# Expert gates applied to rows as they leave PSUM, and expert outputs added into x by accumulating DMAs

## The reference

```
def hier_moe(h, w_rg, w_re, w_gate, w_up, w_down):
    ...
    top_v, top_j = lax.top_k(le_g, TOPK_IN_GROUP)
    gates = p_grp[:, None] * jax.nn.softmax(top_v, axis=-1)
    expert_id = g_sel[:, None].astype(jnp.int32) * EXPERTS_PER_GROUP + top_j.astype(jnp.int32)
    return routed_experts(xt, expert_id, gates, w_gate, w_up, w_down).reshape(B, T, D)

def routed_experts(xt, expert_id, gates, w_gate, w_up, w_down):
    ...
        return (jax.nn.silu(xb @ w_gate[e]) * (xb @ w_up[e])) @ w_down[e]
    ...
    y_assign = y_rows[dest] * gate_sorted[:, None].astype(y_rows.dtype)
    return jnp.zeros_like(xt).at[tok_sorted].add(y_assign)

# per layer:  x = x + hier_moe(rmsnorm(x, norm_ffn[layer]), ...)      at the end:  y = rmsnorm(x, norm_final)
```

## Time and profile before

| | us |
|---|---|
| median of three timed runs (1150.72 to 1150.90) | 1150.72 |
| the profiled execution | 1152.18 |
| its span, first to last instruction | 1150.3 |
| PE busy (4396 matmuls) | 926.5 |
| DVE busy | 358.8 |
| ACT busy | 279.5 |
| POOL busy (266 instructions) | 203.9 |

### The profile page before, as it was taken

The page is one execution under the profiler, slowest core; times in us unless marked ns, Lnnn a source line. Parts: engine busy times, 40 slices in busy tenths (PEclk is TensorE's granted clock), DMA queues, the critical chain, the costliest instruction groups (busy, mean ns, idle before and its releaser), DMA issues.

```text
span 1150.3 us, 12314 instructions
## 1 busy us (share of the span) xinstructions
PE 926.5 (81%) x4396; PEld 510.1 (44%) x4396; DVE 358.8 (31%) x903; ACT 279.5 (24%) x590; POOL 203.9 (18%) x266
## 2 busy tenths in 40 slices
PE   6999979999829987887837998999749978778750
PEld 4566545455514432332315776877524433233220
DVE  3048994443351111000129139202431110010017
ACT  4132234455311111111125322332201111011012
POOL 0000810000011211111133433550011221111110
PEclk9999999999959999988977999999859998998995
DMA  8210143300469999999973420242569999999936
GB/s 274 74 58 1 58 147 128 141 19 20 189 254 367 362 420 422 420 422 420 413 267 99 151 80 9 74 146 111 225 269 412 379 418 421 421 421 419 386 132 238
DMA packets 66679, 278.65 MB, mean 242 GB/s; under 512 B 15837, under 2 KB 22877, under 8 KB 40138
## 3 DMA queue, kind: packets, MB, share of 16 engines
q1 hardware_dynamic: 56842, 259.16, 57.1%
q0 software_dynamic: 9792, 18.90, 4.4%
HBM read 268.76 MB, written 26.03 MB: 256 GB/s over the span
## 4 chain that ended last, share of the span: by engine, by line
PE 56%; DMA 23%; DVE 9%; ACT 4%; POOL 4%; issue 3%; SPq 1%; POOLq 0%; ACTq 0%; DVEq 0%
DMA ring<-in_moe_w_up 20%; PE bank L1599 15%; PE bank L1323 12%; PE bank L1334 11%; PE bank L1300 5%; PE bank L1612 4%; PE bank L1382 3%; PE bank L1446 1%; PE bank L1494 1%; POOL mid L545 1%; DVE x L1237 1%; DVE mid L954 1%; SPq L361 1%; PE bank L1461 1%; ACT mid L652 1%
## 5 line engine op out<-in xcount | busy, mean ns | idle before, releaser
L1599 PE MATMUL bank<-ring,mid 128*64 128x512 f32 x992 | 242.9, 646 | 61.5 <-DMA ring<-in_moe_w_up 57.6
L1599 PEld LDWEIGHTS bank<-ring,mid 128*64 128x64 f32 x992 | 81.9, 149 | 219.3 <-issue 205.7
L652 ACT ACTIVATE mid<-bank 128x512 f32<-128x512 f32 (+6 forms) x182 | 84.7, 508 | 265.1 <-PE bank L1612 124.1
L1300 PE MATMUL bank<-con,mid 128*128 128x128 f32 (+3 forms) x654 | 102.4, 297 | 53.9 <-DVE mid L954 37.7
L1300 PEld LDWEIGHTS bank<-con,mid 128*128 128x128 f32 (+3 forms) x654 | 85.2, 186 | 101.0 <-issue 50.3
L1612 PE MATMUL bank<-ring,mid 128*64 128x512 f32 x496 | 113.3, 597 | 18.6 <-issue 12.9
L1206 DVE TENSOR_TENSOR mid<-mid,bank 128x256 f32<-128x256 f32 x32 | 13.5, 421 | 310.0 <-ACT mid L849 310.0
L1334 PE MATMUL bank<-dw,hT 128*128 128x402 f32 (+1 forms) x384 | 106.3, 461 | 0.6 <-PE bank L1334 0.6
L1323 PE MATMUL bank<-dw_high,hT_high 128*128 128x512 f32 (+1 forms) x240 | 95.9, 399 | 2.6 <-POOL dw_low L582 1.7
L1323 PE MATMUL bank<-dw_low,hT_high 128*128 128x512 f32 (+1 forms) x240 | 94.1, 392 | 0.0
L1323 PE MATMUL bank<-dw_high,hT_low 128*128 128x512 f32 (+1 forms) x240 | 93.9, 391 | 0.0
(11 more groups left out here) (181 smaller groups left out, 951.7 us busy)
## 6 DMA issues: line engine op xcount, KB each, us to landing
ring<-in_moe_w_gate SPq DMA_DIRECT2D x62, 1024.0 KB, 13.1
ring<-in_moe_w_up SPq DMA_DIRECT2D x62, 1024.0 KB, 16.5
ring<-in_moe_w_down SPq DMA_DIRECT2D x62, 1024.0 KB, 18.4
dw<-in_gm_w_in SPq DMA_DIRECT2D x4, 2048.0 KB, 20.0
ring<-y_rows SPq DMA_DIRECT2D x8, 1024.0 KB, 8.0
dw<-in_par_w_in SPq DMA_DIRECT2D x4, 1608.0 KB, 9.1
dw<-in_par_w_out SPq DMA_DIRECT2D x2, 2048.0 KB, 8.4
hT<-in_moe_w_down SPq DMA_DIRECT2D x4, 1024.0 KB, 11.2
```

The costliest lines, as they stand in the source:

```text
L652: return act.activation(dst, src, ACT.Copy, scale=scale)
L1300: return pe.transpose(dst, src, ident[0:k, 0:k])
L1599: ins = pe.matmul(ps[2 + b][64 * k:64 * k + 64, :].rearrange("p (w n) -> p w n", w=2), xT[:, b, c, 64 * k:64 * k + 64], w[:, k, :, c, :], ...
```

## The change

Gates now go in where a pair leaves PSUM, and the combine is left to DMAs:

- SP's `store_gates(l)` writes `gates` to HBM (`gate_rows`, two floats a row, the order of `y_rows`), from SBUF in runs of 8 bytes. It stands between `third_pair`'s two halves in layer 0 and behind them in layer 1.
- POOL gathers for each pair the 128 gates of its slots (4 bytes each) into `gp[:, b]`, with the same index as the scatter's (`gate_index`, `gather_gates`). For the first two pairs it waits for the store; in the loop these stand behind the scatter.
- DVE's copy of `yb` becomes a multiplication by `gp[:, b]`, ACT's copy takes it as its scale; both wait for that gather (`s_gp`).
- SP's loads of `y_rows` go. POOL issues two accumulating DMAs for each tile of x, which add the rows of `y_rows` for choice 0 and for choice 1 into x in SBUF; the second of a tile waits for the first. DVE's `combine` only waits for both and counts `s_res`.
- In an overflow pair POOL gathers the next one's gates after its scatter has landed, and waits for them.

The diff, without declarations:

```diff
@@ -416,11 +423,12 @@
                 sp.wait_ge(s_dwf, 6 * (l + 1) + 1 - k)
                 gate_ups(l, 4, wgu[2], s_wgu[l][2], (k,))
 
-            def combine(l):
-                sp.wait_ge(s_moe[l], 1)
-                for j in range(NT):
-                    sp.dma_start(cb[0:ROWS[j], j], y_rows[l][2 * T0[j]:2 * (T0[j] + ROWS[j]), :]
-                                 .rearrange("(p k) n -> p k n", k=2)).then_inc(s_cl[j], 16)
+            def store_gates(l):
+                sp.wait_ge(s_gat, l + 1)
+                sp.dma_start(gate_rows[l][0:2 * TP, :].rearrange("(j p k) o -> p j (k o)", p=P, k=2), gates[:, 0:4, :],
+                             allow_slow_non_contiguous=True).then_inc(s_gst, 16)
+                sp.dma_start(gate_rows[l][2 * TP:2 * T, :].rearrange("(p k) o -> p (k o)", k=2), gates[0:TS, 4, :],
+                             allow_slow_non_contiguous=True).then_inc(s_gst, 16)
 
             sp.dma_start(x[:, 0, :], a["x_prompt"][0, 0:P, :]).then_inc(s_xl[0], 16)
             load_gain(0)
@@ -469,12 +477,13 @@
             store_rows(1, 0, range(4, NT))
             gate_ups(0, 2, wgu[1], s_wgu[0][1], (1,))
             third_pair(0, 1)
+            store_gates(0)
             for b in range(2):
                 sp.wait_ge(s_xg[0][b], 16)
             third_pair(0, 0)
             load_gain(2)
             experts(0)
-            combine(0)
+            sp.wait_ge(s_moe[0], 1)
 
             for b in range(2):
                 sp.dma_start(*((lng, a["gm_ln_g"][0].partition_broadcast(P)) if b else
@@ -500,13 +509,13 @@
             store_rows(3, 1, range(3, NT))
             gate_ups(1, 2, wgu[1], s_wgu[1][1], (0,))
             third_pair(1, 0)
+            store_gates(1)
             for b in range(2):
                 sp.wait_ge(s_xg[1][b], 16)
             gate_ups(1, 2, wgu[1], s_wgu[1][1], (1,))
             downs(1, 4, wdn[2], s_wd[1][2])
             load_gain(4)
             experts(1)
-            combine(1)
             for j in range(NT):
                 sp.wait_ge(s_h, 4 * NT + j + 1)
                 dst = out[0][0, T0[j]:T0[j] + P, :] if j < 4 else out[1][0]
@@ -530,6 +539,7 @@
             pool.memset(eps[:, 1:2], 1e-5).then_inc(s_eps, 1)
             link(pool.memset(cell[:, :], 0.0))
             pool.memset(line[:, :, 0:HIST], 0.0).then_inc(s_pz, 1)
+            link(pool.memset(gp[:, :, :], 0.0))
 
             link(pool.memset(index[:, 0, 0:P], 0.0))
             pool.memset(index[0:64, 0, 64:P], FAR).then_inc(s_m0, 1)
@@ -568,6 +578,14 @@
                 pool.indirect_dma_start(xg[:, b, :], None, h_rows[l], bass.IndirectOffsetOnAxis(ap=gix[:, b, 0:1], axis=0),
                                         bounds_check=T - 1, oob_is_err=False).then_inc(signal or s_xg[l][b], 16)
 
+            def gate_index(l, i, b):
+                pool.tensor_copy(pix[:, b, :], tab[:, bass.ds(i, 1), :].rearrange("p a v -> p (a v)")).then_inc(s_gcr[l], 1)
+                carry(s_gcr[l], 2 * l, 2 * i + 1)
+
+            def gather_gates(l, b, signal, at):
+                pool.indirect_dma_start(gp[:, b, :], None, gate_rows[l], bass.IndirectOffsetOnAxis(ap=at[:, b, 1:2], axis=0),
+                                        bounds_check=2 * T - 1, oob_is_err=False).then_inc(signal, 16)
+
             def scatter(l, i, b, n):
                 pool.wait_ge(s_yea, i + 1 + PAIRS * l)
                 pool.wait_ge(s_yed, i + 1 + PAIRS * l)
@@ -594,16 +612,24 @@
                 pool.wait_ge(s_tp, NT * (2 * l + 2))
                 gather(l, 0, 0, 0)
                 gather(l, 1, 1, 1)
+                pool.wait_ge(s_gst, 32 * (l + 1))
+                for b in range(2):
+                    gate_index(l, b, b)
+                    gather_gates(l, b, s_gp[b], pix)
 
                 def step(i, b):
                     gather(l, i + 2, b, 2 * i + 2, i + 1)
                     scatter(l, i, b, 2 * i + 3)
+                    gate_index(l, i + 2, b)
+                    gather_gates(l, b, s_gp[b], pix)
 
                 with pool.Fori(0, PAIRS // 2 - 1) as r:
                     step(2 * r, 0)
                     step(2 * r + 1, 1)
                 gather(l, PAIRS, 0, 2 * PAIRS - 2, PAIRS - 1, o_xg[l])
                 scatter(l, PAIRS - 2, 0, 2 * PAIRS - 1)
+                gate_index(l, PAIRS, 0)
+                gather_gates(l, 0, o_gp[l], pix)
                 scatter(l, PAIRS - 1, 1, 2 * PAIRS)
 
                 pool.wait_ge(s_ovf, l + 1)
@@ -628,13 +654,27 @@
                         pool.wait_ge(o_sc[l], 16 * m + 16)
                         pool.wait_ge(o_xg[l], 16 * m + 32)
                         carry(o_cry[l], 2 * l + 1, 7 * m + 7)
-                        pool.nop().then_inc(o_fr[l], 1)
+                        gather_gates(l, 0, o_gp[l], gix)
+                        pool.wait_ge(o_gp[l], 16 * m + 32)
+                        pool.tensor_tensor(cell[:, 6:7], cell[:, 4:5], cell[:, 5:6], ALU.add).then_inc(o_fr[l], 1)
                 with pool.Else():
                     pass
                 for b in range(2):
                     pool.wait_ge(s_sc[l][b], 16 * PAIRS // 2)
                 pool.wait_ge(o_xg[l], 16)
+                pool.wait_ge(o_gp[l], 16)
                 pool.nop().then_inc(s_moe[l], 1)
+
+                def add_rows(j, k):
+                    src = y_rows[l][2 * T0[j]:2 * (T0[j] + ROWS[j]), :].rearrange("(p k) n -> p k n", k=2)[:, k, :]
+                    pool.dma_start(x[0:ROWS[j], j, :], src, accum_op=ALU.add).then_inc(s_cl[j], 16)
+
+                add_rows(0, 0)
+                for j in range(NT):
+                    if j + 1 < NT:
+                        add_rows(j + 1, 0)
+                    pool.wait_ge(s_cl[j], 32 * l + 16)
+                    add_rows(j, 1)
                 if l == 0:
                     weights_low(7)
                     for j in range(NT):
@@ -850,9 +890,10 @@
                     if not (last and b == 1):
                         turned(i + 1, 1 - b, first and b == 0)
                     act.wait_ge(s_dd, i + 1 + PAIRS * l)
+                    act.wait_ge(s_gp[b], 16 * (g + 1 + HALF_PAIRS * l))
                     if not first:
                         act.wait_ge(s_sc[l][b], 16 * g)
-                    copy(yb[:, b, 512:1024], ps[7][:, :]).then_inc(s_yea, 1)
+                    copy(yb[:, b, 512:1024], ps[7][:, :], gp[:, b, :]).then_inc(s_yea, 1)
 
                 act.wait_ge(s_gat, l + 1)
                 turned(0, 0, True)
@@ -875,7 +916,8 @@
                         act.activation(sg, ps[2][:, 0:FE], ACT.Silu).then_inc(o_sg[l], 1)
                         act.wait_ge(o_d[l], m + 2)
                         act.wait_ge(o_fr[l], m + 1)
-                        copy(yb[:, 0, 512:1024], ps[7][:, :]).then_inc(o_y[l], 1)
+                        act.wait_ge(o_gp[l], 16 * m + 16)
+                        copy(yb[:, 0, 512:1024], ps[7][:, :], gp[:, 0, :]).then_inc(o_y[l], 1)
                 with act.Else():
                     pass
 
@@ -1209,9 +1251,10 @@
                         dve.wait_ge(s_dd, i - 1 + PAIRS * l)
                     dve.tensor_copy(hhT[:, b], ps[4][:, 0:256].rearrange("p (c n) -> p c n", c=2)).then_inc(s_hte, 1)
                     dve.wait_ge(s_dd, i + 1 + PAIRS * l)
+                    dve.wait_ge(s_gp[b], 16 * (g + 1 + HALF_PAIRS * l))
                     if not first:
                         dve.wait_ge(s_sc[l][b], 16 * g)
-                    dve.tensor_copy(yb[:, b, 0:512], ps[6][:, :]).then_inc(s_yed, 1)
+                    dve.tensor_scalar(yb[:, b, 0:512], ps[6][:, :], gp[:, b, :], None, ALU.mult).then_inc(s_yed, 1)
                 pair(0, 0, 0, True)
                 pair(1, 1, 0, True)
                 with dve.Fori(1, PAIRS // 2) as r:
@@ -1227,17 +1270,15 @@
                         dve.tensor_copy(hhT[:, 0], ps[4][:, 0:256].rearrange("p (c n) -> p c n", c=2)).then_inc(o_hte[l], 1)
                         dve.wait_ge(o_d[l], m + 2)
                         dve.wait_ge(o_fr[l], m + 1)
-                        dve.tensor_copy(yb[:, 0, 0:512], ps[6][:, :]).then_inc(o_y[l], 1)
+                        dve.wait_ge(o_gp[l], 16 * m + 16)
+                        dve.tensor_scalar(yb[:, 0, 0:512], ps[6][:, :], gp[:, 0, :], None, ALU.mult).then_inc(o_y[l], 1)
                 with dve.Else():
                     pass
 
             def combine(l, j):
                 r = ROWS[j]
-                dve.wait_ge(s_cl[j], 16 * (l + 1))
-                link(dve.scalar_tensor_tensor(x[0:r, j, :], cb[0:r, j, 0, :], gates[0:r, j, 0:1], x[0:r, j, :],
-                                              ALU.mult, ALU.add))
-                dve.scalar_tensor_tensor(x[0:r, j, :], cb[0:r, j, 1, :], gates[0:r, j, 1:2], x[0:r, j, :],
-                                         ALU.mult, ALU.add).then_inc(s_res, 1)
+                dve.wait_ge(s_cl[j], 32 * (l + 1))
+                dve.nop().then_inc(s_res, 1)
 
             route(0)
             experts(0)
```

9 lines of the change are left out of this document (8 added, 1 removed).

## The result

The changed kernel takes 1189.43 us (median of 4 runs, 1187.76 to 1193.64) against 1150.72 for the kernel before: 1.0345 times as long, 95% interval 1.0316 to 1.0374. The direction was predicted; the time lies 20.8 us above the forecast and 3.4 us above the end of the range.

What follows compares the result with a forecast made beforehand. No engine was taken to bound the whole span; the chain of waits was 56% TensorE and 23% DMA. Terms 11.9 + 0.7 + 3.3 + 2 = +17.9 us on 1150.7 gave 1168.6 us, range 1155 to 1186.

Steps and rivals of the forecast that it cites:

- The path: Hand-over from layer 0's experts to the gMLP: POOL reaches `weights_low(7)` only after its last add, +11.9 us.
- The overflow's gate gather: Layer 1's overflow pair: POOL gathers the next gates after the scatter and waits, +3.3 us on the path (2.5 to 4.5).
- I: POOL's cost to issue one accumulating DMA in the combine: taken as 1.55 us, bounds 0.5 and 1.55.
- rival 5: Early expert pairs: gates come late and TensorE stalls, +3 to +8 us on top, 1172 to 1178; chance 0.03.
- l: Combine: an add's landing time after its issue ends, 4.0 us in the tail, 4.7 in layer 0; bounds 2.2 and 8.5.
- rival 1: Combine: adds land as fast as plain transfers, 2.3 to 3.2 us; +6 to +11, 1157 to 1162; chance 0.19.
- the same walk: Combine: schedule of POOL's ten adds by issue and landing; POOL free at 20.9 us, last tile whole at 24.3 (tail).
- rival 2: Combine: adds slower than two plain streams, landing in 5.5 to 7.5 us; 1176 to 1190 us; chance 0.16.
- Rivals 3 and 4: Combine: cheap issue and fast landing, 1143 to 1146 (0.07); or layer 0's loss and tail's gain cancel, 1149 to 1152 (0.05).
- Part 3: Expert loops, gates per slot: small gather packets in the DMA-bound pairs cost +2 us, upper bound 16.
- part 4: SP's store of the gates, 10 to 14 us in a nearly empty queue: costs nothing, upper bound +2.
- The end: After the last tile of x is whole: square, root, scaling and store stay the same, 0 us.

Runs made afterwards that it cites:

- the gates alone: The changed kernel with the old combine: SP loads y_rows and VectorE sums, gates still applied per slot; 1160.75 us, 1.0089 times before.
- the adds alone: The kernel before with ten accumulating DMAs on POOL replacing SP's loads and VectorE's sums, no gate applied anywhere; 1179.57 us, 1.0246 times before.

## Why the prediction was right in direction and short in size

**What held.** The path: POOL's ten adds run one after the other ahead of `weights_low(7)`, and the gMLP waits for it. From `weights_low(7)`'s start to the product I had 8.95 + 2.56 + 0.24 = 11.75 us; it took 11.70 (626.02 to 637.72). The move of the weights gave back 7.3 us, which shows that this order is the path. The overflow's gate gather, +3.3, measured +2.9 in the gates alone; the +3.4 of the changed kernel has some 0.5 of issue ahead of POOL's first add in it, which I had counted in I. The gates came in time, so rival 5 did not come: the store landed some 4.5 us after its issue for four tiles and 6.8 for the last, earlier than my 10 to 14, and no engine waits for a gate gather in the first pairs.

**The step that failed: l, the landing of an add.** I took 4.0 us (4.7 in layer 0) from rows of small scatters and added 1.25 us for reading the destination. It measured 7.2 in the median: 8.1 us from the start of the issue (4.0 for the quickest, 11.8 for the slowest) less the 0.9 of the issue. The ratio was right: an added byte costs two moved ones. Two things were missing. I gave each add this time alone, while two to four are in flight and share engines that are full; ten adds of 4.72 MB need 23.0 us at 205 GB/s whatever their order, and no such sum of bytes stood in my working. In layer 0 SP's loads take a quarter of the engines besides, for which I had added 0.7 us an add. And the base was too low: plain moves from POOL in the same order land after 5.8 us, 5.3 of it behind the issue, where rival 1's plain landing has 2.3. Neither the 2.6 us of SP's store nor the scatter's 2.2 showed that.

**An error on the other side hid some 8 us of it.** I = 1.55 us was too high: adds are issued 0.84 to 0.95 us apart, so one of my signs of being wrong, issues under 0.9 us, came in part; the 0.54 us of issue that I added from the earlier trace rows appears only ahead of a first one, and 0.28 behind a wait. With I = 0.9 the same walk gives POOL free after 18.9 us in layer 0 (l = 4.7; the sum had 22.9) and the last tile whole after 20.2 in the tail (l = 4.0; the sum had 24.3), a forecast 8.1 us lower still. With I = 0.9 and the measured l = 7.2 it gives 26 and 33. Measured from the same point, POOL was free 29.1 us after the scatters were in (626.02 less 596.77 + 0.17), and in the tail the last tile was whole 30.9 us after the first issue. So the walk held and its two terms were off, in opposite directions.

**The rivals.** What came nearest is rival 2, l = 5.5 to 7.5, with its reason against ("the queues are all but empty then") refuted: the adds themselves fill them, at a share of 0.93 to 1.03. An added byte costs as much as two moved ones, though, not more, and l is long because the adds share the engines. Its range, 1176 to 1190, holds the measured 1189.43, in part by luck: it has the dear I of 1.55 and no more than 2 us for the loops. It had 0.16, and the range ended at 1186, inside it. Rival 1 was far off, and the rule of the Trainium skill beside it ("DMA: Bandwidth & Descriptors", Anatomy of one DMA — SWDGE (gpsimd) path), an estimate of 3.2 us for 512 KB, gives less than every landing in the trace: 4.0 us at least for adds and 3.6 for plain moves. Rivals 3 and 4 failed by l; I, at 0.84 to 0.95, was near the 0.9 that they asked for.

**Part 3, the gates in the loops.** I chose +2 between 2 and 16. From the second pair's down product (368.12 in the earlier trace rows) to the last scatter, layer 0 and then layer 1, it is 224.8 and 239.6 us in the changed kernel and 223.3 and 240.9 with the gates alone, against 221.8 and 239.1 before: 3.5 and 3.3 us more. With the adds alone, where no gate is gathered, it is 221.9 and 237.9, so single traces differ by a microsecond. The chosen +2 was a little low and the lower of its bounds the nearer one.

The rest of the 6.5 us in the table's two stretches with loops lies outside the loops: 2.0 at the start of the layers (part 4, next), less 0.3 by which layer 0's first gather of rows is issued earlier, and 1.4 in the gMLP. Of that 0.9 is its first product, 7.67 us where it ran 6.74. That is TensorE's clock. Its stretch before and after (columns as in the windows above; the granted clock is the third number from the end):

```profile
616.18:622.92 6.74, 6.74 (x26) 5.51 (x27) 6.57 (x8) 3.22 (x7) 2.67 (x1) 0.84 0.00 0
637.72:645.39 7.67, 7.67 (x26) 6.22 (x27) 5.76 (x9) 0.00 (x0) 2.18 (x1) 0.73 0.00 0
```

In the changed kernel TensorE idles 9.52 us just ahead of the product, waiting for POOL, and 0.33 before; the product then runs longer at the lower of the clock's two levels, 1.2 GHz: nine matmuls of 0.63 us and more where there were four. No term of mine had a price for that.

**Part 4, the gates' store, +2.0 against 0.** I followed the store to the gathers of pairs 0 to 2 and missed the one transfer on the path while it runs, the first gather of rows. In the chain of waits of the kernel before and of the changed one:

```profile
336.30 4.52 DMA mid<-h_rows,gix
```

```profile
335.99 6.31 DMA mid<-h_rows,gix
```

In the changed kernel SP issues the stores at 337.89 and 338.31, just then, and TensorE waits for this gather. It takes 6.2 us with the gates alone, and 4.28 with the adds alone, which store no gates: so the store makes it 1.8 us longer in layer 0. In layer 1 the same gather takes 4.14 before, 5.76 in the changed kernel, 5.48 with the gathers doubled, 4.24 with the gates alone and 4.12 with the adds alone; there it was hit in two of three kernels. TensorE gets part of this back in the changed kernel, since the product that starts later finds the clock up for more of its length: 8.41 us at a granted 0.84 in both layers, against 9.34 at 0.76 and 8.93 at 0.79 before. From the issue of that gather to the second pair's down product it is 0.9 us longer in layer 0 (335.99 to 368.69, and 336.30 to 368.12 before) and 1.1 in layer 1, 2.0 together. "A nearly empty queue" was no reason for nothing, since what it holds at that moment is what the next stage waits for.

**The end, +0.3 against 0.** This held: the norms of tiles 3 and 4 stand behind the last tile in either kernel, 7.3 us of work before and 7.6 here. VectorE normalizes tile 2 between the landings of tile 3 (1176.1) and tile 4 (1178.3), so that costs no time.

**Left open.** Why an added byte costs two, by a read of x or otherwise, no run separates. Nor is it known why ten plain loads of POOL's take longer than SP's five, or what the gates cost in the loops by packets, by POOL's time and by the clock.
